# Modulation rows moved from a matmul in the inversion stage to dot products on VectorE in the gate stage

## The reference

```python
def ada_split(cond, w_mod, b_mod):
    m = jax.nn.silu(cond) @ w_mod + b_mod          # c: (1, 1024), w_mod: (1024, 6144)
    return jnp.split(m, 6, axis=-1)

sh1, sc1, gt1, sh2, sc2, gt2 = ada_split(c, w_mod, b_mod)
hx  = rms_norm(x, g_pre_mix) * (1.0 + sc1) + sh1          # front stage
zx  = hx @ w_in                                           # project and gate stages
...
gates = jax.nn.sigmoid(zx[..., SHIFT_COLS + D_B:] + b_gate)
m     = gates[..., :D] * ya + gates[..., D:] * yb         # yb: box means of z, w_pool, w_b_out
x     = x + gt1 * rms_norm(m @ w_o, g_post_mix)           # first use of gt1
hx2   = rms_norm(x, g_pre_ffn) * (1.0 + sc2) + sh2
x     = x + gt2 * rms_norm(peer_ffn(hx2, ...), g_post_ffn)
```

## Time and profile before

| | us |
|---|---|
| median of 3 runs | 2924.93 (2923.62 to 2926.19) |
| the profiled execution's own time | 2919.25 |
| its span in the profile | 2917.6 |
| busy: TensorE matmul | 2215.9 (76%) |
| busy: VectorE | 1730.8 (59%) |
| busy: ScalarE | 859.6 (29%) |
| busy: GpSimd | 721.5 (25%) |
| gate stage | about 578 to 727 |
| inversion stage | about 728 to 981 |

### The profile page before, as it was taken

How to read it: one execution, slowest core, us unless ns; L and a number is a source line. 1 busy time by engine, 2 the same in 40 slices (tenths; PEclk the granted TensorE clock), 3 DMA queues, 4 the chain that set the end, 5 groups by cost and what they waited for, 6 DMA issues and landing times. The chain is left out here.

```text
span 2917.6 us, 41994 instructions
## 1 busy us (share of the span) xinstructions
PE 2215.9 (76%) x16681; PEld 1386.4 (48%) x16681; DVE 1730.8 (59%) x3472; ACT 859.6 (29%) x1718; POOL 721.5 (25%) x607
## 2 busy tenths in 40 slices
PE   5667667398767688887888898878777777777876
PEld 2645545187642677876665454333333332333332
DVE  2367767642582033433556666877777777777764
ACT  4244444232442323332332222222122212221221
POOL 0000000080000111111004333444444444444441
PEclk8888888699768699998999999999999999999898
DMA  3222322342523433230539999999999999999995
GB/s 159 69 88 86 148 109 86 143 150 81 225 99 124 176 140 133 90 140 17 187 128 399 363 384 342 421 411 420 421 420 420 421 421 420 420 421 421 421 421 220
DMA packets 119316, 741.36 MB, mean 254 GB/s; under 512 B 16065, under 2 KB 23265, under 8 KB 48353
## 3 DMA queue, kind: packets, MB, share of 16 engines
q0 software_dynamic: 73728, 536.90, 44.7%
q1 hardware_dynamic: 44256, 199.88, 18.5%
q10 hardware_dynamic: 1152, 2.10, 0.2%
HBM read 683.14 MB, written 55.69 MB: 253 GB/s over the span
## 5 line engine op out<-in xcount | busy, mean ns | idle before, releaser
L2278 PE MATMUL bank<-uv,dg 128*128 128x512 f32 x1664 | 810.4, 644 | 232.3 <-ACT dg L2086 227.4
L2278 PEld LDWEIGHTS bank<-uv,dg 128*128 128x128 f32 x1664 | 333.7, 205 | 699.6 <-issue 408.9
L2171 DVE SCALAR_TENSOR_TENSOR junk<-uv,gr 128x1024 f32<-128x1024 f32 x416 | 509.9, 1226 | 219.1 <-DMA uv<-in_uv_in,ic 193.3
L2009 POOL DMA_INDIRECT uv<-in_uv_in,ic x416 | 461.0, 1108 | 663.3 <-PE bank L2278 584.7
L2081 ACT ACTIVATE ge<-dt_ 128x4 f32<-128x4 f32 x128 | 26.5, 207 | 927.5 <-DVE junk L2171 927.4
L91 PE MATMUL bank<-ht_hi,wh 128*128 128x256 f32 (+1 forms) x432 | 164.4, 381 | 110.0 <-DVE wl L477 73.9
L2278 PE MATMUL bank<-uvx,dg 128*128 128x512 f32 x384 | 190.3, 653 | 56.5 <-ACT dg L2086 56.5
L2086 ACT ACTIVATE dg<-ident,gc_ 128x128 f32<-128x128 f32 x512 | 164.2, 392 | 29.4 <-DVE gc_ L2177 29.2
L91 PEld LDWEIGHTS bank<-ht_hi,wh 128*128 128x128 f32 x432 | 96.0, 222 | 136.3 <-issue 102.2
L92 PE MATMUL bank<-ht_lo,wh 128*128 128x256 f32 (+1 forms) x432 | 158.5, 367 | 0.0
L2278 PEld LDWEIGHTS bank<-uvx,dg 128*128 128x128 f32 x384 | 78.1, 209 | 168.7 <-issue 92.3
(11 more groups left out here) (357 smaller groups left out, 3982.9 us busy)
## 6 DMA issues: line engine op xcount, KB each, us to landing
pair_record<-rec SPq DMA_DIRECT2D x8, 4364.0 KB
wm<-in_wmod SPq DMA_DIRECT2D x16, 1024.0 KB, 5.1
wraw<-in_wpair_in SPq DMA_DIRECT2D x8, 1536.0 KB, 14.9
ab<-pair_record SPq DMA_DIRECT2D x16, 768.0 KB, 6.3
wz<-in_wz_in SPq DMA_DIRECT2D x20, 512.0 KB, 3.5
wm<-in_wmod SPq DMA_DIRECT2D x4, 2048.0 KB, 21.4
wraw<-in_wq_in SPq DMA_DIRECT2D x16, 512.0 KB
uv<-in_uv_in,ic POOLq DMA_INDIRECT x416
```

The costliest lines, as they stand in the source:

```text
L2009: pool.indirect_dma_start(ring(i), None, g["uv_in"], bass.IndirectOffsetOnAxis(ap=ic[:, s % ICR, k:k + 1], axis=0)).then_inc(su[row_slot[i ...
L2171: dve.scalar_tensor_tensor(junk[:, :], ring(i)[:, 0:D], 1.0, hc[:, t % 2, :], ALU.mult, ALU.mult, accum_out=dt[:, k:k + 1]).then_inc(s_ud, 1)
L2278: mm = pe.matmul(acc(t, c)[:, :], dg[:, n % 2, k, :], ring(i)[:, D + 512 * c:D + 512 * c + 512], start=h == 0 and q == 0 and k == 0, stop= ...
```

## The change

The four late rows leave the inversion. `halves`, `row`, `column` and `columns` go from it, with their waits. In the gate stage the same numbers are made as 32 x 128 dot products along the free axis: the host lays w_mod's last 4096 columns out by column (`wrow_in`, 32 tiles of 128 x 1024, 512 KB each), SyncE broadcasts c to all partitions (512 KB) and loads tile m into one of two buffers wt, ScalarE and VectorE make silu(c) once (sd), and VectorE's `dot(m)` multiplies a tile by it with an accumulator output into one column of mc. VectorE does dots 2n − 4 and 2n − 3 in its iteration n (n = 2 to 17) behind the low part of tile n. SyncE issues wt tiles 2n − 2 and 2n − 1 in its iteration n, behind wz(n), each from the third on behind a wait for the dot that used its buffer, m − 2. `columns` comes in VectorE's last iteration, the transpose on TensorE and the copy on ScalarE before the y products, and SyncE stores the rows and waits for that store before its loop of the y products. The y weights wb keep two tiles of eight in SBUF: two loads of 256 KB at n = 4, the others in the y loop, each behind the split of the tile that had the buffer.

```diff
@@ -662,18 +662,31 @@
 
 
 def gates(nc, sb, sem, g):
-    gv, bank, ht_hi, ht_lo, ga_dram, gb_dram = (g[k] for k in ("gv", "bank", "ht_hi", "ht_lo", "ga_dram", "gb_dram"))
+    gv, bank, ident, ht_hi, ht_lo, ga_dram, gb_dram, rows_dram = (g[k] for k in (
+        "gv", "bank", "ident", "ht_hi", "ht_lo", "ga_dram", "gb_dram", "rows_dram"))
     NW = len(WINDOWS)
     PAD = max(WINDOWS) // 2
     PR, PC = ROWS + 2 * PAD, GRID_W + 2 * PAD
     NZ = NW + 2 * NPAIR
+    NM, MR = 4 * KT, 2
     with ExitStack() as st:
+        wt = sb(st, "wt", [P, MR, D])
+        cb_ = sb(st, "cond", [P, D])
+        sd = sb(st, "cond_silu", [P, D])
+        mc = sb(st, "mod_dots", [P, NM])
+        colv = sb(st, "colv", [P, 4, KT])
+        rw = sb(st, "rw", [NM, P])
+        s_wt = [sem(st, f"row_weights{k}_loaded") for k in range(MR)]
+        s_cb, s_cth, s_si, s_dot, s_cv, s_ct, s_rw, s_rst, s_chm = (sem(st, n) for n in (
+            "cond_loaded", "cond_tanh", "cond_ready", "mod_dot", "columns_scaled", "mod_columns_turned", "rows_copied", "rows_stored",
+            "dve_chain_r"))
         p_hi = sb(st, "p_hi", [P, NW, SEQ], F32R)
         p_lo = sb(st, "p_lo", [P, NW, SEQ], F32R)
         wz = sb(st, "wz", [P, 2, KT, P])
         wzh = sb(st, "wzh", [P, 2, KT, P], F32R)
         wzl = sb(st, "wzl", [P, 2, KT, P], F32R)
-        wb = sb(st, "wb", [P, NPAIR, NW, P])
+        wb = sb(st, "wb", [P, 2, NW, P])
+        s_wb = [sem(st, f"yb_weights{b}") for b in range(2)]
...
+        def dot(dve, m):
+            if m >= NM:
+                return
+            dve.wait_ge(s_wt[m % MR], 16 * (m // MR) + 16)
+            if m:
+                dve.wait_ge(s_dot, m)
+            dve.scalar_tensor_tensor(cb_[:, :], wt[:, m % MR, :], 0.5, sd[:, :], ALU.mult, ALU.mult,
+                                     accum_out=mc[:, m:m + 1]).then_inc(s_dot, 1)
+
+        def columns(dve):
+            ch = Chain(dve, s_chm)
+            dve.wait_ge(s_dot, NM)
+            for v, q in enumerate((0, 2, 1, 3)):
+                o = GV_BMOD + 16 + 8 * q
+                ch(dve.tensor_tensor(colv[:, v, :], mc[:, 8 * q:8 * q + 8], gv[:, o:o + 8], ALU.add))
+            ch(dve.tensor_tensor(colv[:, 0, :], colv[:, 0, :], gv[:, GV_GPOM:GV_GPOM + 8], ALU.mult))
+            ch(dve.scalar_tensor_tensor(colv[:, 1, :], colv[:, 1, :], 1.0, gv[:, GV_GPF:GV_GPF + 8], ALU.add, ALU.mult))
+            dve.tensor_tensor(colv[:, 3, :], colv[:, 3, :], gv[:, GV_GPOF:GV_GPOF + 8], ALU.mult).then_inc(s_cv, 1)
...
-                        sp.dma_start(wb[:, :, :, :], g["wb_in"]).then_inc(s_wb, 16)
+                        for b in range(2):
+                            sp.dma_start(wb[:, b, :, :], g["wb_in"][:, b, :, :]).then_inc(s_wb[b], 16)
+                    if n == 1:
+                        sp.dma_start(cb_[:, :], g["c_in"].broadcast_to((P, D))).then_inc(s_cb, 16)
+                    for m in range(2 * n - 2, 2 * n):
+                        if 0 <= m < NM:
+                            if m >= MR:
+                                sp.wait_ge(s_dot, m - MR + 1)
+                            sp.dma_start(wt[:, m % MR, :], g["wrow_in"][m]).then_inc(s_wt[m % MR], 16)
+                sp.wait_ge(s_rw, 1)
+                sp.dma_start(rows_dram.rearrange("v (k p) -> (v k) p", p=P), rw[:, :]).then_inc(s_rst, 16)
+                sp.wait_ge(s_rst, 16)
                 for j in range(NPAIR):
+                    if j + 2 < NPAIR:
+                        sp.wait_ge(s_bh, j + 1)
+                        sp.wait_ge(s_bl, j + 1)
+                        sp.dma_start(wb[:, j % 2, :, :], g["wb_in"][:, j + 2, :, :]).then_inc(s_wb[j % 2], 16)
                     sp.wait_ge(s_gy, j + 1)
                     sp.dma_start(gb_dram[j], gy[:, j % 2, :]).then_inc(s_bs[j % 2], 16)
...
                 high(0)
                 high(1)
+                act.wait_ge(s_cb, 16)
+                act.activation(sd[:, :], cb_[:, :], ACT.Tanh, scale=0.5).then_inc(s_cth, 1)
                 act.wait_ge(s_z0, NW + 2)
...
-                act.wait_ge(s_wb, 16)
+                act.wait_ge(s_ct, 1)
+                act.activation(rw[:, :], bank[6][0:NM, 0:P], ACT.Copy).then_inc(s_rw, 1)
                 for j in range(NPAIR):
+                    act.wait_ge(s_wb[j % 2], 16 * (j // 2) + 16)
                     if j >= 2:
                         act.wait_ge(s_yb, j - 1)
-                    act.activation(wbh[:, j % 2, :, :], wb[:, j, :, :], ACT.Copy).then_inc(s_bh, 1)
+                    act.activation(wbh[:, j % 2, :, :], wb[:, j % 2, :, :], ACT.Copy).then_inc(s_bh, 1)
...
                     dve.wait_ge(s_hi, n + 1)
                     dve.tensor_tensor(wzl[:, n % 2, :, :], wz[:, n % 2, :, :], wzh[:, n % 2, :, :].bitcast(FP32),
                                       ALU.subtract).then_inc(s_lo, 1)
+                    if n == 1:
+                        dve.wait_ge(s_cth, 1)
+                        dve.scalar_tensor_tensor(sd[:, :], sd[:, :], 1.0, cb_[:, :], ALU.add, ALU.mult).then_inc(s_si, 1)
+                        dve.wait_ge(s_si, 1)
+                    if n >= 2:
+                        dot(dve, 2 * n - 4)
+                        dot(dve, 2 * n - 3)
+                    if n == NZ - 1:
+                        columns(dve)
                     if n >= NW + 2 and n % 2 == 0:
                         half_gate(dve, (n - NW) // 2 - 1)
...
+                pe.wait_ge(s_cv, 1)
+                pe.transpose(bank[6][0:NM, 0:P], colv[:, :, :].rearrange("p v k -> p (v k)"), ident[:, :]).then_inc(s_ct, 1)
                 pe.wait_ge(s_plo, NW)
...
-                def halves(n):
-                    for i in range(2):
-                        if n:
-                            sp.wait_ge(s_rp, 2 * n - 1 + i)
-                        sp.dma_start(wm[:, i, :, :], g["wmod"][4 + n][:, i * 2048:i * 2048 + 2048].rearrange(
-                            "p (k n) -> p k n", k=KT // 2)).then_inc(s_wm[i], 16)
-
                 for j in range(NPAIR):
                     if j >= 2:
                         sp.wait_ge(s_t, 4 * (j - 1))
                     for i, o in enumerate((RC_A, RC_B)):
                         sp.dma_start(ab[:, j % 2, i, :, :, :], record[j, :, o:o + NDIR * T].rearrange(
                             "p (d c s) -> p d c s", d=NDIR, c=NC)).then_inc(s_ab[j % 2], 16)
-                for n in range(EARLY + 1):
-                    halves(n)
                 stored(0)
-                for n in range(EARLY + 1, NR):
-                    halves(n)
-                sp.wait_ge(s_rw, 1)
-                sp.dma_start(rows_dram.rearrange("v (k p) -> (v k) p", p=P), rw[:, :]).then_inc(s_rs, 16)
                 stored(1)
...
-                for n in range(EARLY):
-                    row(n)
                 turned_out(0)
                 combined(0)
-                for n in range(EARLY, NR):
-                    row(n)
-                act.wait_ge(s_ct, 1)
-                act.activation(rw[:, :], bank[7][0:4 * KT, 0:P], ACT.Copy).then_inc(s_rw, 1)
                 turned_out(1)
...
-                        if b and u == HB - 10:
-                            columns()
                     dve.sem_inc(s_inv, 1)
...
-                    pe.wait_ge(s_rwc, NR if b else EARLY)
-                    if b:
-                        pe.wait_ge(s_rw, 1)
...
-                pe.wait_ge(s_ric, 32)
-                for n in range(EARLY):
-                    row(n)
                 turned_out(0)
                 combined(0)
-                pe.wait_ge(s_zc, 12)
-                column(0)
-                for n in range(EARLY, NR):
-                    row(n)
-                    column(n - 1)
-                column(NR - 1)
-                pe.wait_ge(s_cv, 1)
-                pe.transpose(bank[7][0:4 * KT, 0:P], colv[:, :, :].rearrange("p v k -> p (v k)"), ident[:, :]).then_inc(s_ct, 1)
                 turned_out(1)
...
-        "x": i["x"], "ctx_in": i["ctx"], "gvec_in": gvec,
-        "wmod": w_mod.reshape(KT, P, MODG, 512).transpose(2, 1, 0, 3).reshape(MODG, P, KT * 512),
+        "x": i["x"], "ctx_in": i["ctx"], "c_in": i["c"], "gvec_in": gvec,
+        "wmod": w_mod[:, :2 * D].reshape(KT, P, 4, 512).transpose(2, 1, 0, 3).reshape(4, P, KT * 512),
+        "wrow_in": w_mod[:, 2 * D:].T.reshape(4 * KT, P, D),
```

More of the change, by code:

```diff
@@ L93, in split_mm, with build @@
     return tensor.matmul(out, w_lo, x_hi, start=False, stop=last)
[L96 removed]
+def build(nc, x, ctx_in, c_in, gvec_in, wmod, wrow_in, wlora_in, wpair_in, pvec_in, lora_in, wz_in, wpool_in,
           invcnt_in, wb_in, wa_in, wo_in, wq_in, keys_in, uv_in, out):
@@ L154, in front @@
 def front(nc, sb, sem, g):
-    gv, mod, sc, ident, blk, bank, ht_hi, ht_lo = (g[k] for k in (
-        "gv", "mod", "sc", "ident", "blk", "bank", "ht_hi", "ht_lo"))
+    gv, mod, ident, blk, bank, ht_hi, ht_lo = (g[k] for k in (
+        "gv", "mod", "ident", "blk", "bank", "ht_hi", "ht_lo"))
     NB = 4
@@ L164, in front @@
         modrow = sb(st, "modrow", [2, NB * 512])
```

(44 more changed lines are left out.)

7 lines of the change are left out of this document (2 added, 5 removed).

## The result

The changed kernel takes 2980.83 us (median of 4 runs, 2974.56 to 2987.29) against 2925.56 (2923.62 to 2927.06) for the kernel before in the same comparison: 1.0189 times as long, interval 1.0166 to 1.0213. The forecast was 2954 with a range of 2936 to 2978: the direction was right, the loss is 55 us in place of 29, and the median lies 2.8 us above the range. The profiled execution took 2982.07 us, its span is 2980.4.

The account below looks back on a forecast made before the run. TensorE was taken to bound the gate stage, VectorE the inversion. −42.9 + 63.7 + 6.5 + 1.7 = +29.0 us on the profiled 2919.25 gives 2948; put against the median, 5.7 higher, 2954 us (1.0% slower), range 2936 to 2978.

Parts of the forecast that it names:

- Inversion, −42.9: Inversion: VectorE's hole in the elimination, waiting for the modulation row's columns, goes wholly; −42.9 us.
- The closed loop: Gate stage: wz(n+1) waits for two dots after tile n's low part; 15 rounds of 9.95 us against 5.44, +63.7.
- The landing: Gate stage: wz, issued at t+3.1 (t: low part's end), lands at t+7.6 behind one wt load, 4.5 after issue.
- The upper bound of t+8.1: Gate stage: latest wz landing after the low part's end, at 1.6 us for each of three transfers; round 10.45.
- GpSimd beside the dots, +6.5: Gate stage until 655: low parts and dots stretched beside GpSimd's box sums, 18 x 0.36 us; bounds 0 and 28.
- The rival of 28 us: Gate stage, shared port: each of 18 VectorE operations loses 1.57 us, 28 in place of 6.5, so 2976; chance 0.07.
- Tail, +1.7: End of the gate stage: columns, transpose, copy (+0.4), rows' store and y weight reloads; +1.7 us in all.
- Late y weights: Gate stage's y loop: weights 3, 5 and 7 come some 0.4 us late each; bounds 0 to 6.
- Overlap (2939): Gate stage rival: the two loads overlap, wz lands 3.5 after issue, round 8.95, 15 us less; chance 0.15.
- The wait that does not bind (2885): Gate stage rival: dots fit VectorE's slack, tiles stay at 5.44, only the inversion's gain less 3 shows; chance 0.04.
- The clock (2972 to 2983): Gate stage rival: TensorE at 1.2 GHz after idling; 2983 if throughout, 2972 if in half the rounds; chance 0.06.
- the tile of 7.1 us: Gate stage: if only a tile's first part runs at low clock, it takes 7.1 us, hidden in the round.

Follow-up runs that it names:

- experiment 4: Changed kernel with the wait for both dots kept before wz, but wz issued first and the two wt loads behind it: 2946.39 us, 1.0076.
- Experiment 1: Changed kernel without the 32 wt loads and the 32 dots, one memset zeroing mc in their place: 2878.14 us, 0.9845.
- experiment 3: Changed kernel with SyncE's iteration n loading wt 2n−4 and 2n−3 in place of 2n−2 and 2n−1: 2902.88 us, 0.9932.
- experiment 6: Changed kernel loading only half the columns of each wt tile from the third on: 2958.69 us, 1.0128.
- experiment 10: Changed kernel loading only the second wt tile of each round, even tiles staying stale: 2956.42 us, 1.0127.
- Experiment 11: Changed kernel with GpSimd's box sums left out: 2966.89 us, 1.0162.
- experiment 7: Changed kernel with wt loads one round later and four wt buffers, broadcast c and junk output in gy's space: 2894.91 us, 0.9913; again 2894.29, 0.992.
- experiment 5: Changed kernel with the wt loads reading the z weights' tensor, same size and order: 2977.2 us, 1.0178.
- experiment 8: Changed kernel with all dots on the first two wt tiles, no further wt loads, and GpSimd's box sums left out: 2882.16 us, 0.9873.
- experiment 2: Changed kernel with all 32 dots on the first two wt tiles, the other loads and their waits for dots left out: 2892.36 us, 0.9885.

## Why the prediction was right, and where it fell short

- *Inversion, −42.9: right, measured −39.8.* The hole closed wholly. 2.1 us were lost ahead of the first elimination (38.95 us from the stage's start, 36.81 before), 0.9 behind the second turning out; neither was tried by an experiment, and the first stretch, untouched by the edits, took from 36.9 (experiment 4) to 39.0 us. Experiment 1, with 213.0, has the same inversion without the dots.
- *The closed loop: right.* 15 rounds, TensorE waiting in 15 of them, wz some 12 us apart, and experiment 3 opens the loop with one index.
- *The landing: the step that failed.* "But wt(2n−1), issued at t+2.7, lands at t+6.2 at the earliest, and the second transfer of a pair lands later by its own data time" counts one load ahead of wz. There were two: wt(2n−2), let go by the first dot 1.8 us before wz, takes longer than that to land. Measured, with what stands ahead of wz (512 KB each; means of tiles 3 to 16, and tile 17 moves them by 0.03 at most):

| ahead of wz in the queue | issue to high part, us | from |
|---|---|---|
| nothing (two behind) | 3.90 | experiment 4 |
| two of half size | 4.38 | experiment 6 |
| one | 4.60 | experiment 10 |
| two | 5.79 | changed kernel |

  5.79 − 4.5 = 1.29 us in each of 15 rounds is 19.4 of the 26.8 us by which the gate stage exceeds the forecast. The upper bound of t+8.1 did reckon with three transfers, at 1.6 each, and is passed as well: 2.9 + 5.79 = 8.7.
- *GpSimd beside the dots, +6.5: the mechanism right, the size low.* Experiment 11 gives 10.0 for the stage, so 3.5 more; in the 15 rounds themselves it is 7.1, close to the term. The mean of all low parts (0.36 each) understates what follows: three VectorE operations in a row, with GpSimd in a row too, each wait out a whole instruction, 2.7 and 2.0 us lost in the two dots above. The rival of 28 us is much further off.
- *Tail, +1.7: measured 4.4* (from the last z tile to the next stage 33.6 us, 29.2 before), 2.7 more. In experiment 1, with the same tail, it is 31.0, which is 1.7 more than before, as forecast. The step said nothing of the clock there, and the first product of the changed kernel met it: 12 matmuls at a granted clock of 0.50 in the window 794 to 800. The same product in the kernel before, by the view of windows, ran at 1.00:

```profile
701.00:705.00 4.00, 3.02 (x13) 2.54 (x14) 1.44 (x3) 0.55 (x2) 0.00 (x0) 1.00 0.00 0
```

  Its start and its taking in the changed kernel, from the timeline:

```profile
794.98 0.77 PE L91 MATMUL bank<-p_hi,wbh 128*128 128x512 f32 x1 [3.40 <-DVE wbl L904]
...
800.48 0.69 DVE L724 SCALAR_TENSOR_TENSOR gy<-tb,bank 128x512 f32<-128x512 f32 x1 [5.04 <-PE bank L93]
```

  5.5 us from its first matmul to its taking, where it had been 3.0. TensorE had been idle for 3.40 us before it; but it had been for 3.44 in the kernel before, and for 3.40 in experiment 1, where the product ran at 1.00 too. So that this product is slow is shown, and why its clock fell is not. Late y weights were forecast three times at 0.4; ScalarE waited for them five times, 13.1 us in all, most of it beside other work.
- 19.4 + 3.5 + 2.7 = 25.6 of the 26.8 us; 1.2 is not assigned. Cut by time instead, 1.0 lies ahead of t(2), 22.7 in the 15 rounds (11.90 each, against 9.95 and the 6.5 beside GpSimd), 0.4 in the last three tiles and 2.7 in the tail.
- *The rivals.* Overlap (2939) fell: 3.5 after issue is about what wz takes with nothing ahead (3.9), not here. The wait that does not bind (2885) fell in the changed kernel, but it is what experiment 7 builds: 2894, with a gate stage 13.4 us over experiment 1's, which is the price of the dots beside the sums. The clock (2972 to 2983) gives a time near the one measured, but not by its mechanism (and its 2972 does not follow from its own terms: half of the rounds and the last three tiles are 2954 + 7 + 15 = 2976). The granted clock is 0.78 and 0.83 in the rounds; the timeline of a tile shows a slow start and then full speed:

```profile
635.53 0.63 PE L92 MATMUL bank<-ht_lo,wzh 128*128 128x512 f32 x1
...
636.38 0.63 PE L91 MATMUL bank<-ht_hi,wzh 128*128 128x512 f32 x1
...
638.05 0.39 PE L91 MATMUL bank<-ht_hi,wzh 128*128 128x512 f32 x1
```

  0.63 us for one, 0.39 from 638 on. That is the tile of 7.1 us that the prediction called hidden, and it was: TensorE still waited 15 times for VectorE's low part, 60.2 us in all.
- *The range* took one case at a time. The landing's upper bound alone would have given 15 x 0.5 = 7.5 more than the forecast, and the landing alone brought 19.4; three terms came out small together, and 2954 + 25.6 is past 2978.

What stays open: why wz behind two loads takes some 1.2 us more than behind one, while the pair at the stage's start was 1.3 apart and landed in step with that. It is not the tensor (experiment 5) nor GpSimd (experiment 11). What a fourth load in flight would do was not tried. Open too is why the clock fell before the first y product.

## What to carry to other kernels

When loads for a second user are put into one engine's queue, ask of each wait there whether its releaser itself needs the next load of that queue: here one index decided between +1.9% and −0.7% for the same bytes and the same arithmetic, and two more buffers brought −0.9%. When such a loop must be priced, count every load that is still in flight at the issue, not only the one just ahead, and put the load that the critical engine waits for first (34 us here). Work moved into an engine's idle time is only free where its reads do not take turns with another engine's: 32 dots cost the z tiles nothing alone (106.9 us from first to last in experiment 8, as before) and 13.4 us beside GpSimd's sums (120.3 in experiment 2).
